# Expert rows finished in their second expert's slot, a weight ring of 20 halves, and shift pieces issued earlier in merging

## The reference

```python
ya = o_a @ w_br_a
yb = y_b @ w_br_b
x = x + (sigmoid(gate_a) * ya + sigmoid(gate_b) * yb) @ w_o
h2 = rmsnorm(x, g_ffn)
g_sel = argmax(h2 @ w_group + b_group)              # 1 of 4 groups of experts
top_val, top_idx = top_k(its 8 experts' logits, 2)   # 2 of 8 experts
out = 0
for e in range(32):
    hid = silu(h2 @ w_gate_e[e]) * (h2 @ w_up_e[e])
    out = out + gates[:, e:e + 1] * (hid @ w_down_e[e])
y = rmsnorm(x + out, g_final)
new_buf = concat(cache[1:], new key and value)       # each sample's window of branch B, moved up by one row
```

## Time and profile before

| what | value |
|---|---|
| median of 3 runs | 1323.79 us (1319.96 to 1324.32) |
| span of the profiled execution (its own time) | 1329.1 us |
| PE busy | 1131.4 us (85%) |
| PE weight loads busy | 664.0 us (50%) |
| DVE busy | 585.7 us (44%) |
| ACT busy | 246.0 us (19%) |
| POOL busy | 274.2 us (21%) |
| DMA, mean over the span | 343 GB/s |
| memory read and written | 442.10 MB and 65.44 MB |

### The profile page before, as it was taken

One profiled execution on the slowest core, in us unless ns is written; L12 is line 12 of the kernel. 1 busy time (PEld: TensorE's weight loads), 2 busy tenths in 40 slices (PEclk: granted clock), 3 DMA queues, 4 the chain that ended last, 5 costly groups with the idle time before them and its releaser, 6 DMA issues. The chain is left out here.

```text
span 1329.1 us, 13696 instructions
## 1 busy us (share of the span) xinstructions
PE 1131.4 (85%) x5474; PEld 664.0 (50%) x5474; DVE 585.7 (44%) x738; ACT 246.0 (19%) x399; POOL 274.2 (21%) x204
## 2 busy tenths in 40 slices
PE   3999999999987999979999739988888888888770
PEld 3877888888854444436646323333333333333320
DVE  3089999999955646524531351111111111111115
ACT  2022111210223544510021101111111111111112
POOL 1035454554311333310000000111111111111110
PEclk9999999999988999988999859999899998898995
DMA  6969999999837899998937487999999999999935
GB/s 197 383 228 392 363 396 367 406 408 408 315 118 279 330 404 415 398 414 324 285 127 264 166 370 257 413 410 411 412 411 412 413 410 410 409 412 409 412 150 208
DMA packets 104342, 455.71 MB, mean 343 GB/s; under 512 B 13613, under 2 KB 45661, under 8 KB 57445
## 3 DMA queue, kind: packets, MB, share of 16 engines
q1 hardware_dynamic: 72469, 301.43, 58.2%
q0 software_dynamic: 24032, 143.60, 27.6%
q10 hardware_dynamic: 7776, 9.78, 2.2%
HBM read 442.10 MB, written 65.44 MB: 382 GB/s over the span
## 5 line engine op out<-in xcount | busy, mean ns | idle before, releaser
L506 PE MATMUL proj_ps<-hT,w_slots 128*128 128x260 f32 x1472 | 330.2, 384 | 4.9 <-ACT stage L529 2.6
L506 PEld LDWEIGHTS proj_ps<-hT,w_slots 128*128 128x128 f32 x1472 | 278.2, 191 | 55.0 <-issue 11.9
L1852 PE MATMUL ex_gp<-raw,ex_xT 128*64 128x512 f32 x672 | 167.9, 648 | 43.5 <-DMA raw<-in_w_up_e 42.7
L206 POOL DMA_INDIRECT ring<-in_cache_k_a,run_sb x64 | 137.7, 2152 | 196.3 <-DVE scores L574 167.9
L1804 DVE TENSOR_TENSOR ex_hm<-ex_sg,ex_gp 64x512 f32<-64x512 f32 x32 | 21.7, 679 | 342.4 <-ACT ex_sg L1783 342.4
L567 DVE TENSOR_TENSOR ring<-ring,q_rep 128x2048 f32<-128x2048 f32 x64 | 145.8, 2280 | 43.0 <-ACT q_rep L551 40.6
L574 DVE TENSOR_REDUCE scores<-ring 128x32 f32<-128x2048 f32 x64 | 145.6, 2276 | 0.0
L1852 PEld LDWEIGHTS ex_gp<-raw,ex_xT 128*64 128x64 f32 x672 | 55.5, 148 | 140.8 <-issue 133.6
L1852 PE MATMUL ex_gp<-qk,ex_xT 128*64 128x512 f32 x352 | 93.1, 680 | 25.8 <-DMA qk<-in_w_up_e 24.7
L1754 POOL DMA_INDIRECT pair_rows<-ex_yg,ex_to x32 | 29.6, 924 | 407.2 <-PE ex_xp L1838 397.2
L206 POOL DMA_INDIRECT ring<-in_cache_v_a,run_sb x64 | 71.5, 1117 | 170.1 <-PE at_vp L774 151.9
(11 more groups left out here) (260 smaller groups left out, 1053.1 us busy)
## 6 DMA issues: line engine op xcount, KB each, us to landing
raw<-in_w_down_e SPq DMA_DIRECT2D x53, 1024.0 KB, 29.3
raw<-in_w_gate_e SPq DMA_DIRECT2D x42, 1024.0 KB, 28.8
raw<-in_w_up_e SPq DMA_DIRECT2D x42, 1024.0 KB, 28.5
o_kvs<-in_cache_kv_b SPq DMA_DIRECT2D x39, 1024.0 KB
w_slots<-in_w_in SPq DMA_DIRECT2D x23, 1024.0 KB, 12.4
qk<-in_w_gate_e SPq DMA_DIRECT2D x22, 1024.0 KB, 28.3
qk<-in_w_up_e SPq DMA_DIRECT2D x22, 1024.0 KB, 28.4
qk<-in_w_down_e SPq DMA_DIRECT2D x11, 1024.0 KB, 29.5
```

What stands on the lines that cost most here:

```text
L206: pool.indirect_dma_start(k.ring[:, n % RING, :], None, runs, bass.IndirectOffsetOnAxis(ap=k.run[:, i:i + 1], axis=0), bounds_check=runs.s ...
L506: last = pe.matmul(pp[:, j, half, 0:H], w[:, m % W_PARTS, c, j * P:(j + 1) * P], k.hT[:, c, half * H:(half + 1) * H], start=(c == 0), stop ...
L1852: last = pe.matmul(gp[at:at + SLOT, j], xT[:, c, :], raw_slot(k, slot)[:, c1 * FF:(c1 + 1) * FF], start=(c == 0), stop=(c == KC - 1))
```

## The change

- **Rows finish in place.** `finish`, its scratch `pairs` and the separate outputs are gone. Experts are now visited in turn through the groups (slot p is expert p % 4 * 8 + p // 4), so that a token's two experts stand at least four slots apart. A scratch `part` holds x for each token at first (copied from the inputs' rows in merging, and then written for the first of the token's two experts). For each expert, the stored rows are the raw x with the reciprocal root in a further column (rows of 1040 numbers, `x_rows`): PE's turning multiplies with a diagonal of these roots, and VectorE lays the result out times `g_ffn`. A token that meets its second expert gets its partial sum from `part` gathered over the raw rows in the same buffer (four buffers now), the result is added, squared, rooted, scaled and stored to the output; a token that meets its first expert has its sum stored to `part`.
- **Ring of 20.** Two further places lie in `scores` and `oT`, loaded in merging behind a new wait for the samples' second branch (`yb_s`).
- **Shift pieces.** The last eight pieces, and ahead of them the copy into `part`, are issued by SP ahead of the wait for `values`.
- **Routing.** Both choices of a token are worked in one set of operations, PE needs three matmuls for the ranks instead of nine, and POOL clears the x buffers and starts the first four gathers within `route`. Counting extra slots moves into `experts`.

The diff, cut to its core:

```diff
-SETS = 3
-RING_W = 6 * SETS
-RAW_EARLY = 5
+RING_W = 20
+RAW_QK = 5
+RAW_EARLY = 7
+ROW = D + 16
+XB = 4
...
                 sp.wait_ge(s["ya"], KC)
-                load_expert(k, sp, 0, 0, some=range(2))
+                for n in range(2):
+                    load_half(k, sp, n)
+                sp.dma_start(k.io["part"][0:SEQ, :], k.io["x_prompt"][0]).then_inc(k.rows_out, 16)
+                sp.dma_start(k.io["part"][SEQ:TOK, :], x_rows(k, NB)).then_inc(k.rows_out, 16)
+                shift(k, sp, shift_pieces()[IN_PROJECT + IN_ATTEND + IN_MERGE:])
                 sp.wait_ge(s["values"], 1)
-                load_expert(k, sp, 0, 0, some=range(2, RAW_EARLY))
-                shift(k, sp, shift_pieces()[IN_PROJECT + IN_ATTEND + IN_MERGE:])
+                for n in range(2, RAW_QK):
+                    load_half(k, sp, n)
+                sp.wait_ge(s["yb_s"], 1)
+                for n in range(RAW_QK, RAW_EARLY):
+                    load_half(k, sp, n)
                 for b in range(NBLK):
                     r = rows_of(b)
                     sp.wait_ge(s["scaled"], b + 1)
-                    sp.dma_start(k.io["h2"][b * P:b * P + r, :], hn(b)[0:r, :]).then_inc(k.h2_out, 16)
+                    sp.dma_start(k.io["x_rows"][b * P:b * P + r, :], k.x1[0:r, b, :]).then_inc(k.rows_out, 16)
...
+def gather_x(k, pool, p):
+    pool.indirect_dma_start(k.xg[:, p % XB, :], None, k.io["x_rows"], bass.IndirectOffsetOnAxis(
+        ap=k.index[:, 0, p:p + 1], axis=0), bounds_check=TOK - 1, oob_is_err=False).then_inc(k.x_in[p % XB], 16)
...
             def _(sp):
-                load_expert(k, sp, 0, 0, some=range(RAW_EARLY, 6))
-                for e in range(1, SETS):
-                    load_expert(k, sp, e, e)
+                for n in range(RAW_EARLY, RING_W):
+                    load_half(k, sp, n)
...
             def _(pool):
+                pool.memset(k.xg[:], 0.0).then_inc(s["cleared"], 1)
                 for sem in done:
                     pool.sem_clear(sem)
+                pool.wait_ge(s["cleared"], 1)
+                pool.wait_ge(s["indexed"], 1)
+                for p in range(XB):
+                    gather_x(k, pool, p)
...
+                def gather_part(p):
+                    pool.wait_ge(s["turned"], p + 1)
+                    pool.wait_ge(a_out[(p - E_GROUPS) % XB], 16 * ((p - E_GROUPS) // XB + 1))
+                    rows(p % XB, x_of(p % XB), k.index[:, 2, p:p + 1], b_in[p % XB])
+                def store_part(p):
+                    pool.wait_ge(s["added"], p + 1)
+                    store("part", k.index[:, 1, p:p + 1], x_of(p % XB), a_out[p % XB])
+                def store_out(p):
+                    pool.wait_ge(s["out"], p + 1)
+                    store("o_y", k.index[:, 2, p:p + 1], yo[:], y_out)
+                for p in range(EXPERTS):
+                    if p >= E_GROUPS:
+                        gather_part(p)
+                    if p >= 2:
+                        store_out(p - 2)
+                        if XB <= p + 2 < EXPERTS:
+                            pool.wait_ge(a_out[(p - 2) % XB], 16 * ((p - 2) // XB + 1))
+                            gather_x(k, pool, p + 2)
+                    if p >= 1:
+                        store_part(p - 1)
+                store_out(EXPERTS - 2)
+                store_out(EXPERTS - 1)
...
+                def root(p):
+                    act.wait_ge(s["added"], p + 1)
+                    if p:
+                        act.wait_ge(s["out"], p)
+                    act.activation(sq[0:SLOT, :], x_of(p % XB), ACT.Square, accum_out=ms[:]).then_inc(s["squared"], 1)
+                    act.wait_ge(s["squared"], p + 1)
+                    act.activation(rms[:], ms[:], ACT.Sqrt, bias=k.const("eps", SLOT), scale=1.0 / D)\
+                        .then_inc(s["roots"], 1)
...
+                def diag(p):
+                    dve.wait_ge(x_in[p % XB], 16 * (p // XB + 1))
+                    if p:
+                        dve.wait_ge(s["turned"], p)
+                    dve.tensor_scalar(dg[:], k.const("ident", SLOT)[:, 0:SLOT], x_of(p % XB, D, D + 1), None, ALU.mult)\
+                        .then_inc(s["diag"], 1)
+                def lay_x(p):
+                    dve.wait_ge(s["turned"], p + 1)
+                    dve.tensor_tensor(xT[:], xp[:], k.g_ffn[:].unsqueeze(2).to_broadcast([P, KC, SLOT]), ALU.mult)\
+                        .then_inc(s["x_laid"], 1)
+                def add(p):
+                    if p >= E_GROUPS:
+                        dve.wait_ge(b_in[p % XB], 16 * ((p - E_GROUPS) // XB + 1))
+                    dve.wait_ge(s["y_high"], p + 1)
+                    gate = k.slot_gate[:, p:p + 1]
+                    lo, hi = x_of(p % XB, 0, 512), x_of(p % XB, 512, D)
+                    dve.scalar_tensor_tensor(lo, yp[0:SLOT, p % 2], gate, lo, ALU.mult, ALU.add)
+                    dve.scalar_tensor_tensor(hi, y2[:], gate, hi, ALU.mult, ALU.add).then_inc(s["added"], 1)
+                def out(p):
+                    dve.wait_ge(s["roots"], p + 1)
+                    if p:
+                        dve.wait_ge(y_out, 16 * p)
+                    link(dve.reciprocal(rstd[:], rms[:]))
+                    dve.scalar_tensor_tensor(yo[:], x_of(p % XB), rstd[:], gf[:], ALU.mult, ALU.mult)\
+                        .then_inc(s["out"], 1)
...
+                for p in range(EXPERTS):
+                    last = p == EXPERTS - 1
+                    if not last:
+                        diag(p + 1)
+                    else:
+                        add(p - 1)
+                        out(p - 1)
+                    hidden(p)
+                    if not last:
+                        lay_x(p + 1)
+                    lay_h(p)
+                    if p and not last:
+                        add(p - 1)
+                        out(p - 1)
+                add(EXPERTS - 1)
+                out(EXPERTS - 1)
...
-STEPS = [prepare, project, attend, merge, route, experts, finish]
+STEPS = [prepare, project, attend, merge, route, experts]
```

697 lines of the change are left out of this document (364 added, 333 removed).

## The result

The changed kernel takes 1395.07 us, the median of 4 runs (1390.93 to 1395.35), beside 1324.05 for the kernel before on the same chip: a ratio of 1.052, 95% interval 1.049 to 1.055. It is **slower by 71 us** where the prediction had 1316, 8 us faster. The profiled execution has a span of 1388.8 us; it was 0.45% under its median, as that of before was 0.4% over its own, so the two spans differ by 59.7 us only.

What follows compares the result with a forecast made beforehand. The weight stream was taken to bound the expert stage, with the final stage running alone at the end. Terms 24.0 - 7.2 - 24.2 = -7.4 on the 1329.1 us span gave 1321.7, or 1316 as a median; range 1292 to 1329.

Steps and rivals of the forecast that it cites:

- the expert stream: Expert stage: extra VectorE and GpSimd work hidden under the stream's 16 us an expert; stage and routing terms sum to -7.2 us.
- The slow rival: Expert stage: one x buffer's chain of store, landing, gather, landing and diagonal sets the pace; 1343 us, chance 0.17.
- experts more than 16.3 us apart with DMA under 400 GB/s: Expert stage: sign set down for the x buffers' chain being the bound, the rival at 1343 us.
- Rows: Expert stage: row gathers and stores priced by bytes, 10.7 MB for 8.5 MB, +5.4 us.
- The third rival: Expert stage: row transfers crowd a part of the engines, so rows cost double, another 5.4 us; 1322, chance 0.10.
- First projection: From routing's first operation to the first projection: 30.9 us instead of 38.0, gathers going out at once and landing in 7.5.
- Routing's count of operations: Routing, up to the first index: short and longer operations plus 2.0 us for PE, 21.1 us.
- the issuing of ScalarE's loads held by a full queue: Merging: shift pieces and copy delay the values' loads, freeing ScalarE at 704.0 instead of 681.83; routing starts 24.0 us later.
- the first rival: Merging: ScalarE's queue is deeper and doesn't hold it; only PE waits, +11.6 instead of +24, 1304 us, chance 0.18.
- the tail's chain from last matmul through the store's issue: After the last expert: copy, additions, square, table load, root, product and store issue take 7.5 us; whole tail -24.2 us.
- The table load: Tail: 1.28 us from the trace, where the skill page gives 2.66 for a switch with its drain; then a gain of 22.8.
- The tail's rest: After the last store's issue: landing and stage end as before, 8.4 us, plus 0.5 for the closing wait.

Runs made afterwards that it cites:

- late_root: Changed kernel with rows turned by transposes of the raw x and the reciprocal root applied behind the projections; ratio 1.023 to the kernel before, span 1352.7 us.
- before_product: Kernel before with rows turned by matrix products with the identity instead of transposes; ratio 1.045 to the kernel before, span +55.0 us.
- upper_rows: best1 plus three small edits, with partial rows gathered into partitions 64 to 127 instead of 0 to 63; ratio 0.998, beside 0.996 without that move.
- no_partial_rows: late_root without the gathers and stores of partial rows; ratio 1.003 to the kernel before, span 1327.0 us.
- best1: Changed kernel with late_root's turning, copy and shift pieces back behind halves 2 to 4, first four gathers at the expert stage's head; ratio 1.0005, span 1322.6 us.
- part_gather_plus: best1 plus three small edits, with one more half-row gather an expert from the fifth on into an unread tile; ratio 0.998, beside 0.996 without it.

## Why the prediction was wrong

**The step that failed** is the sentence in the expert stream: "If that cover went, PE's own work would be next: 7.09 + 2 x 1.89 and two short turnings, near 12.6". The turning was taken as short because eight instructions of 64 columns were, without asking whether it was still the same instruction. A transpose had become a float32 product, and that took 4.02 us for 1.1 and left the next projection 1.7 us slower by the clock. TensorE's need came out at 16.95 us an expert, above the 16.2 of the stream, and since it holds from the first expert on, the three experts' weights already in place bought nothing. late_root takes 36.1 us off by going back to transposes, and before_product, with nothing else changed, puts 55 on the kernel before. The slow rival that I did write down, the chain of the x buffers, was the wrong mechanism: PE waited for no rows at all, and the landings stayed at 6.7 to 7.4 us. The sign set down for it, experts more than 16.3 us apart with DMA under 400 GB/s, came true all the same (16.95 and 379), so it couldn't tell that rival from a slow TensorE; PE's list of waits can.

The Trainium skill (FP8 and Floating Point Precision, TensorE Precision Notes) says that a true float32 product goes through the array in four passes. The measured factor, 4.02 to 1.10 or 3.7, is near that, though the trace lists two matmuls for each product. Their 16 weight loads fill 3.9 of the 4.0 us, where the eight of the transposes take 0.96, so whether passes or loads set the time isn't shown. By four passes the turning would be 4.4 us and PE's sum 15.9, an estimate and still under the stream's 16.2: the rule warns of the turning, but only the 1.7 us by the clock carry the sum over.

**Rows.** The prediction priced rows by their bytes, +5.4 for 10.7 MB in place of 8.5. The partial rows alone, 4.3 MB, cost 25.7 us with the stream as the bound, where their bytes at 410 GB/s make 10.4. The third rival had "rows cost double" but for a reason that upper_rows refuted. In the changed kernel itself TensorE's longer need covers this term: before_product has no partial rows, and its stage is no shorter (550.0 us for 545.7).

**First projection.** "The gathers go out at once, 7.5 to landing": they did go out at once, at 801.2, but the block that holds them was left at 816.5. This made 6.4 us of the 10.7 by which this stretch missed; 2.9 more are the longer first turning.

**Held.** Routing's count of operations (20.2 for 21.1 us); the issuing of ScalarE's loads held by a full queue (701.6 for 704.0), the first rival's opposite, though its price was right by two errors, which is luck; the tail's chain from last matmul through the store's issue (8.1 for 7.5). The table load took 1.28 us and the root began 0.02 behind it, so the row was the right one to take. The 2.66 us that the Trainium skill (ScalarE: Activation LUTs, What ACT_TABLE_LOAD costs) has for a switch with its drain doesn't show here. The tail's rest was mis-sized: 13.2 us for 8.9. It was taken as in the kernel before, but GpSimd's drain at the stage's end takes 9.8 us now where it took 5.6 (last section).

The pieces of the miss, 59.7 + 7.4 = 67.1 us on the spans: 36.1 turning; 15.3 partial rows beyond their bytes (25.7 - 10.4), which show only once the turning is taken away; 6.4 gathers; 5.0 end; less 2.4 in merging: in sum 60. The other 7 are not settled.

## What to carry to other kernels

When an operand that was a constant becomes data, look up which form of the instruction is left: a turning by identity and a turning by a diagonal look alike in the code and differed by 3.7 here. A scale per row can often wait until the rows are on partitions again, where ScalarE's scale and VectorE's fused product take it for under 0.1 us each (in late_root 0.68 us for 0.59 and 0.75 for 0.68). A stream-bound stage is no licence: TensorE had 4 us of slack an expert, and the edit took 2.9 directly and 1.7 by the clock.

## What was not expected

- **GpSimd leaves a block late after row transfers.** Its drain took 13.7 us in routing, ending 0.8 us behind the gathers' last packet (815.5), and 9.8 at the end of the changed kernel, where the last store's packets had all landed by 1376.9, 1.5 us before it began. At the end of the expert stage its length goes with the number of row transfers issued in the stage: 4.9 us for 60 (no_partial_rows), 5.6 for 66 (before), 7.6 for 92, 7.8 for 95, 9.8 for 119 (the changed kernel) and 10.1 for 123 (best1), some 0.08 us each. So nearly all of the tail's 4.3 us goes with its 53 further transfers. part_gather_plus, 3.4 us for 151, doesn't fit. No run was made to test this count, and what the drain does in that time isn't shown.
- **Gathered bytes are dear.** 2.1 MB gathered to 64 partitions took 17 to 20 us from a stream of 390 GB/s, 2.1 MB stored took 5 to 6. It isn't decided by the number of rows, by the memory read or by the partitions; bytes and packets remain. With partial rows the weight queue moves 19015 packets in 370 us at a share of 94.7%, without them 19772 at 97.0%, so a packet takes 295 ns for 290 and the queue has less of the engines' time.
- **A copy and a shift of the same kind of queue differ.** 2.1 MB of whole rows ahead of the values' loads cost nothing; 7.3 MB of shift pieces cost 23 us. No run put 2.1 MB of pieces there, so kind and size aren't told apart.
